# Feed-forward products on the unscaled input, with the token scale multiplied in when banks are emptied

## The chip, the core and the metric

The kernel runs on one core of a Trainium2 chip. The metric is the time of one execution on the device in microseconds (us). A core has five engines with a queue each: PE (TensorE) multiplies matrices, ACT (ScalarE) evaluates functions, DVE (VectorE) does elementwise work, POOL (GpSimd) does elementwise work and issues DMAs here, and SP only issues DMAs. They run side by side and wait for one another by semaphores.

## What is computed

Two layers of a decoder work on 256 prompt tokens and 8 x 8 sample tokens, 320 in all. What matters here is the end of a layer:

```python
x = x + rms_norm(merged @ w_o, g_mix_post)
h2 = rms_norm(x, g_ffn_pre)
f = (jax.nn.silu(h2 @ w_ffn_gate) * (h2 @ w_ffn_up)) @ w_ffn_down
x = x + rms_norm(f, g_ffn_post)
```

`rms_norm(x, g)` is `x * rsqrt(mean(x*x) + EPS) * g`: one scale for each token, one gain for each channel. The model width is 1024 and the feed-forward width is 2816, all in float32.

## The kernel before

**Layout.** Channels lie on the 128 partitions and the 320 tokens along the free dimension. `x` is 8 tiles of 128x320 (`KT` = 8), a feed-forward activation is 22 tiles (`FT` = 22). A matrix is cut into *units* of up to eight 128x128 weight tiles; the layer has 180, numbered in the order in which they are used: `U_WO` = 104 (8 units of `w_o`), `U_GU` = 112 (44 units, gate and up in turn), `U_DOWN` = 156 (24 units).

**Units.** Each unit's weights come by one 512 KB DMA from SP into one of four ring slots (`wring`). ACT rounds them to `whi`, DVE forms the rest `wlo = wring - whi`, and PE multiplies three ways (`whi*hi`, `whi*lo`, `wlo*hi`) for each of the eight tiles: 24 matmuls of 320 columns into one of banks 0 to 3. The activations are split likewise into `hhi` and `hlo`. `split(l, u)` on ACT and DVE prepares unit u + 3 (`AHEAD` = 3), so it also waits until PE has finished unit u - 1.

**The norm ahead of the feed-forward.** ACT squares the products of `w_o` (L888), PE averages the squares over channels with a matrix of ones into bank X (L449, L454), and ACT makes `rstd` from that with Ln and Exp (L774, L781). DVE multiplies the products with it and adds to `x`, two tiles at a time (L1374, L1376). ACT squares the new `x` (L992), PE averages again (L468 in `stat`), ACT makes the next `rstd`, DVE forms `acc = x * gain * rstd` (L1043 in `normalised`), ACT rounds this to `hhi` (L894), and DVE forms `hlo` (L1025 in `lower`). `keep_clock` (L444) issues matmuls whose result nobody reads, 20 ahead of the average and 12 behind it.

**The first units.** `first_units` works on units 0, 1 and 2 of `U_GU` together: for each k it waits until `h_ready` says that `hlo` tile k is there, and then issues nine matmuls. Unit 3 follows through `unit`, and then the loop over the other 40. I call them unit 0 to unit 43 of the feed-forward.

**The banks of the feed-forward.** For each n, ACT takes the sigmoid of the gate's bank (L793), DVE multiplies the bank with it (L1393), and then multiplies with the up projection's bank (L1399). The result is rounded to `fhi` (L999) and `flo`. Each engine's order is written out by hand, and so is every wait.

Of the kernel before, what the change touches and what calls it, by code (L numbers as in the profile page):

```python
# [53 lines left out]
ROPES, CONVS, POSTS = 12, TAPS, 16  # L54
# [34 lines left out]
def program(nc, w, xin, consts, params, r_in, c_in, x_out, rp_out, rs_out, cp_out, cs_out):  # L89
    ctx = ExitStack()  # L90
    with ctx:
# [101 lines left out]
        sq_paired = sem("sq_paired")  # L193
        stat_read = sem("stat_read")
# [60 lines left out]
        def _(pool):  # L255
# [137 lines left out]
            for n in range(0, KT, 2):  # L393

                pool.wait_ge(post_step, (DEPTH - 1) * POSTS + (8 + n + 2))
                pool.dma_start(x_out[:, n:n + 2, :], x[:, n:n + 2, :]).then_inc(x_stored, 16)
# [6 lines left out]
        def _(pe):  # L403
# [244 lines left out]
            for l in range(DEPTH):  # L648
# [75 lines left out]
                keep_clock(20)  # L724
                pe.wait_ge(stat_read, l * STATS + (ST_POST + 1))
                stat(l, 0, lambda k: sq8[:, k, :], KT, ones_d,
                     lambda k: pe.wait_ge(sq_done, l * SQS + (SQ_FFN + k + 1))).then_inc(stat_done, 1)

                keep_clock(12)
                first_units(l, U_GU // RING, lambda k: h_read(l, 8 + k))  # L730
                unit(l, U_GU // RING, AHEAD, AHEAD, h_tile)
# [22 lines left out]
        def _(act):  # L754
# [135 lines left out]
            def halves_of_h(l, sub):  # L890

                for k in range(KT):
                    act.wait_ge(h_value, l * 16 + (8 * sub + k + 1))
                    act.activation(hhi[:, k, :], acc[:, k, :], ACT.Copy).then_inc(h_hi, 1)  # L894
# [19 lines left out]
            for l in range(DEPTH):  # L914
                act.wait_ge(stat_done, l * STATS + 1)
                rsqrt(l, X[:, 0:T], 0, 0)
                halves_of_h(l, 0)
# [72 lines left out]
                for k in range(KT):  # L990
                    act.wait_ge(post_step, l * POSTS + (k // 2 * 2 + 2))
                    act.activation(sq8[:, k, :], x[:, k, :], ACT.Square).then_inc(sq_done, 1)  # L992
                act.wait_ge(stat_done, l * STATS + (ST_FFN + 1))
                rsqrt(l, X[:, 0:T], ST_FFN, RS_FFN)
                halves_of_h(l, 1)
# [5 lines left out]
                for n in range(FT):  # L1001
                    split(l, U_GU + 2 * n)
                    if n >= 4:
                        act.wait_ge(ffn_step, l * (2 * FT) + (2 * (n - 4) + 1))
                    gemm(l, U_GU + 2 * n)
                    sigmoid(sig[:, n % 4, :], bank[(2 * n) % 4][:, 0:T])
# [9 lines left out]
                for k in range(KT):  # L1016
                    act.wait_ge(post_step, l * POSTS + (8 + k // 2 * 2 + 2))
# [4 lines left out]
        def _(dve):  # L1022
# [15 lines left out]
            def normalised(l, sub, rs, gain):  # L1038

                dve.wait_ge(rstd_done, l * RSTDS + (rs + 1))  # L1040
                for k in range(KT + 2):
                    if k < KT:
                        dve.scalar_tensor_tensor(out=acc[:, k, :], in0=x[:, k, :], scalar=g_(gain + k), in1=rstd[:, :],  # L1043
                                                 op0=ALU.mult, op1=ALU.mult).then_inc(h_value, 1)
                    if k >= 2:
                        dve.wait_ge(h_hi, l * 16 + (8 * sub + k - 1))
# [202 lines left out]
            for l in range(DEPTH):  # L1249
                dve.wait_ge(par_loaded, l * 16 + 16)  # L1250
                normalised(l, 0, 0, G_MIXPRE)
# [107 lines left out]
                def post(sub, rs, sq0, gain, u0, ustep):  # L1359
# [145 lines left out]
```

## Time and profile before

| | |
|---|---|
| median of 3 runs | 1571.06 us (1570.09 to 1571.96) |
| profiled execution, its own time | 1572.03 us |
| span in the profile (first to last instruction) | 1570.2 us |
| PE busy | 1513.2 us, 96% |
| DVE busy | 1111.0 us, 71% |
| ACT busy | 674.3 us, 43% |
| POOL busy | 290.9 us, 19% |
| mean granted TensorE clock | 0.992 of full speed |

A busy PE may be doing nothing useful: the matmuls of `keep_clock` count as busy. The layers follow each other in time; the norm treated here stands at 541 to 555 us in the first and at 1309 to 1322 us in the second.

### The profile page before, as it was taken

Reading aid. Unit: us, or ns where it says so; the run is one execution under the profiler, and the core shown is the slowest. Engines: PE = TensorE matmul, PEld = TensorE weight load, DVE = VectorE, ACT = ScalarE, POOL = GpSimd, SP = SyncE. Lnnn points to the kernel's source line nnn. Section 1 sums busy time; section 2 is a strip of 40 time slices with the busy share of each in tenths; the row PEclk is TensorE's granted clock in tenths of the full one; section 3 lists DMA queues with packets and bytes.
Section 4 is the critical chain, followed back from the end, with each engine's and each line's share of the span. In section 5 each row is a group of like instructions: output and inputs, shape, how many; then the busy total and the mean of one; then the engine's idle time right before and its main releaser. Section 6 shows DMA issues by size and latency. Waiting matters only on the chain.

```text
span 1570.2 us, 25591 instructions
## 1 busy us (share of the span) xinstructions
PE 1513.2 (96%) x9840; PEld 1401.2 (89%) x9840; DVE 1111.0 (71%) x1735; ACT 674.3 (43%) x993; POOL 290.9 (19%) x257
## 2 busy tenths in 40 slices
PE   6999999999999999999999999999989999999997
PEld 5997878787899999999999978788779998999997
DVE  7789989987657567654466988989785665655544
ACT  3433434346355453434343344345454544443433
POOL 6974000101110029910000300101021000000000
PEclk8999999999999999999999999999999999999999
DMA  6554755646344434444444555748544442544443
GB/s 254 174 196 160 268 214 213 242 173 245 121 159 138 156 121 146 149 149 159 161 152 166 178 215 215 253 186 298 183 173 153 132 152 68 173 148 147 154 158 116
DMA packets 64541, 275.48 MB, mean 175 GB/s; under 512 B 7233, under 2 KB 7233, under 8 KB 55233
## 3 DMA queue, kind: packets, MB, share of 16 engines
q1 hardware_dynamic: 52560, 192.17, 36.7%
q0 software_dynamic: 11888, 82.04, 13.9%
q8 instruction: 62, 1.02, 0.3%
q14 instruction: 31, 0.25, 0.0%
HBM read 230.30 MB, written 43.89 MB: 175 GB/s over the span
## 4 chain that ended last, share of the span: by engine, by line
PE 82%; DVE 12%; ACT 4%; issue 1%; DMA 0%; DVEq 0%; ACTq 0%
PE bank L415 24%; PE bank L416 23%; PE bank L417 23%; DVE acc L1060 3%; DVE wlo L1025 2%; PE bank L602 2%; PE bank L580 1%; DVE state L1091 1%; PE bank L563 1%; PE bank L435 1%; DVE acc L1043 1%; ACT L770 1%; PE bank L516 1%; DVE tmp L1080 1%; DVE x L1376 1%
## 5 line engine op out<-in xcount | busy, mean ns | idle before, releaser
L415 PE MATMUL bank<-hhi,whi 128*128 128x320 f32 x2016 | 654.6, 325 | 7.8 <-DVE wlo L1025 7.8
L1025 DVE TENSOR_TENSOR wlo<-wring,whi 128x1024 fp32r<-128x1024 f32 x363 | 473.0, 1305 | 221.2 <-ACT whi L763 199.1
L417 PE MATMUL bank<-hhi,wlo 128*128 128x320 f32 x2016 | 625.7, 310 | 0.0
L416 PE MATMUL bank<-hlo,whi 128*128 128x320 f32 x2016 | 625.1, 310 | 0.0
L415 PEld LDWEIGHTS bank<-hhi,whi 128*128 128x128 f32 x2016 | 381.1, 189 | 39.3 <-issue 36.7
L416 PEld LDWEIGHTS bank<-hlo,whi 128*128 128x128 f32 x2016 | 381.4, 189 | 8.6 <-issue 7.7
L763 ACT ACTIVATE whi<-wring 128x1024 fp32r<-128x1024 f32 x264 | 278.1, 1055 | 240.5 <-PE bank L417 240.0
L417 PEld LDWEIGHTS bank<-hhi,wlo 128*128 128x128 f32 x2016 | 380.8, 189 | 0.0
L1060 DVE SCALAR_TENSOR_TENSOR acc<-up,par,acc 128x256 f32<-128x256 f32 x480 | 209.6, 504 | 0.2
L789 ACT ACTIVATE whi<-wring 128x1024 fp32r<-128x1024 f32 x96 | 101.2, 1054 | 72.1 <-PE bank L417 71.6
L793 ACT ACTIVATE sig<-bank 128x320 f32<-128x320 f32 x92 | 40.2, 437 | 202.0 <-PE bank L417 188.0
L415 PE MATMUL bank<-fhi,whi 128*128 128x320 f32 x352 | 110.4, 314 | 0.0
L417 PE MATMUL bank<-fhi,wlo 128*128 128x320 f32 x352 | 108.5, 308 | 0.0
L416 PE MATMUL bank<-flo,whi 128*128 128x320 f32 x352 | 108.5, 308 | 0.0
L1091 DVE SCALAR_TENSOR_TENSOR state<-state,con,bank 128x512 f32<-128x512 f32 x128 | 89.8, 743 | 12.5 <-PE bank L580 11.4
L299 POOL DMA_DIRECT2D rs_out<-state x32 | 17.4, 543 | 387.5 <-DVE state L1091 387.5
L392 POOL DMA_DIRECT2D par<-params x2 | 1.2, 578 | 465.0 <-DVE acc L1368 465.0
L415 PE MATMUL bank<-ghi,whi 128*128 128x320 f32 x256 | 78.9, 308 | 2.5 <-DVE glo L1025 2.5
L416 PE MATMUL bank<-glo,whi 128*128 128x320 f32 x256 | 78.8, 308 | 0.0
L417 PE MATMUL bank<-ghi,wlo 128*128 128x320 f32 x256 | 78.7, 308 | 0.0
L1393 DVE TENSOR_TENSOR tmp<-bank,sig 128x320 f32<-128x320 f32 x44 | 21.6, 491 | 70.5 <-ACT sig L793 70.5
L416 PEld LDWEIGHTS bank<-flo,whi 128*128 128x128 f32 x352 | 66.1, 188 | 0.6
(157 smaller groups left out, 1953.4 us busy)
## 6 DMA issues: line engine op xcount, KB each, us to landing
wring<-w SPq DMA_DIRECT2D x364, 512.0 KB, 3.7
state<-r_in POOLq DMA_DIRECT2D x32, 1024.0 KB, 7.6
rs_out<-state POOLq DMA_DIRECT2D x32, 1024.0 KB, 4.9
rp_out<-pst POOLq DMA_DIRECT2D x8, 512.0 KB, 7.7
us<-c_in POOLq DMA_DIRECT2D x2, 1216.0 KB, 5.5
cs_out<-us POOLq DMA_DIRECT2D x2, 1216.0 KB, 9.4
cp_out<-up POOLq DMA_DIRECT2D x2, 1144.0 KB, 5.9
con<-consts POOLq DMA_DIRECT2D x1, 1420.0 KB, 9.0
```

Source lines behind the costliest of these rows:

```text
L299: pool.dma_start(rs_out[H * QUADS + q], state[q % 2][:, :, :]).then_inc(r_stored[q % 2], 16)
L415: pe.matmul(bank[g][:, 0:T], whi[j][:, k, :], hi, start=start and k == 0, stop=False)
L416: pe.matmul(bank[g][:, 0:T], whi[j][:, k, :], lo, start=False, stop=False)
L417: mm = pe.matmul(bank[g][:, 0:T], wlo[j][:, k, :], hi, start=False, stop=stop and k == n - 1)
L602: mm = pe.matmul(aux[pos % 3][:, :], kdec[:, c, d * P:(d + 1) * P], vtok[:, c, :], start=(c == 0), stop=(c == 1))
L763: act.activation(whi[s][:, :, :], wring[s][:, :, :], ACT.Copy).then_inc(hi_done, 1)
L789: act.activation(whi[s][:, :, :], wring[s][:, :, :], ACT.Copy).then_inc(hi_done, 1)
L793: act.activation(dst, src, ACT.Sigmoid).then_inc(sig_done, 1)
L1025: return dve.tensor_tensor(dst, value, hi.bitcast(F32), ALU.subtract)
L1060: dve.scalar_tensor_tensor(out=out, in0=src, scalar=tap, in1=out, op0=ALU.mult, op1=ALU.add).then_inc(conv_step, 1)
L1091: dve.scalar_tensor_tensor(out=st, in0=st, scalar=con[:, ds(hd + C_CD, 1)], in1=aux[pos % 3][:, :], op0=ALU.mult, op1=ALU.add).then_inc(dv ...
L1393: dve.tensor_tensor(tmp[:, n % 4, :], bank[b][:, 0:T], sig[:, n % 4, :], ALU.mult).then_inc(ffn_step, 1)
```

## The change

Now the gain is multiplied into `x` on the way to `hhi` and `hlo`, and the scale of each token is left out of the products. A product of the feed-forward input is therefore too large or small by one factor for each token, and DVE multiplies this factor in when it reads the banks. Since the first units no longer need `rstd`, the squares are summed while they run.

The `x` update goes in groups of 1, 1, 2, 2 and 2 tiles. The eight averaging matmuls become four, since DVE first adds the squares in pairs (`add_squares`); two stand in `first_units` behind k = 5, two in unit 3 behind k = 3. The 20 `keep_clock` matmuls are gone and the 12 stay. The preparation of unit 3 moves ahead of the `x` groups on ACT, and behind them on DVE. The gate's Sigmoid becomes a Silu on an SBUF tile that DVE has scaled, and DVE has three operations for each n where it had two.

```diff
@@ -51,7 +51,10 @@
-ROPES, CONVS, POSTS = 12, TAPS, 16
+ROPES, CONVS, POSTS, POSTS0 = 12, TAPS, 18, 10
+MIX_GROUPS = ((0, 1), (1, 1), (2, 2), (4, 2), (6, 2))
@@ -437,6 +442,8 @@
                         mm = pe.matmul(bank[j][:, 0:T], wlo[j][:, k, :], hhi[:, k, :], start=False, stop=(k == UB - 1))
                         if k == UB - 1:
                             mm.then_inc(unit_done, 1)
+                    if between is not None:
+                        between(k)
             def keep_clock(n):
@@ -721,14 +728,19 @@
                          ready=(lambda k: pe.wait_ge(m_ready, l * 8 + (k + 1))) if n == 0 else None,
                          between=lambda k: square_means(l, 0, SQ_POST, n, k))
                 square_mean(l, SQ_POST, KT - 1).then_inc(stat_done, 1)
-                keep_clock(20)
-                pe.wait_ge(stat_read, l * STATS + (ST_POST + 1))
-                stat(l, 0, lambda k: sq8[:, k, :], KT, ones_d,
-                     lambda k: pe.wait_ge(sq_done, l * SQS + (SQ_FFN + k + 1))).then_inc(stat_done, 1)
                 keep_clock(12)
-                first_units(l, U_GU // RING, lambda k: h_read(l, 8 + k))
-                unit(l, U_GU // RING, AHEAD, AHEAD, h_tile)
+                def half_mean(i):
+                    pe.wait_ge(sq_halves, l * 2 + (i + 1))
+                    if i == 0:
+                        pe.wait_ge(stat_read, l * STATS + (ST_POST + 1))
+                    for k in (4 * i, 4 * i + 1):
+                        mm = pe.matmul(X[:, 0:T], ones_d[:, :], sq8[:, k, :], start=(k == 0), stop=(k == 5))
+                    return mm
+                first_units(l, U_GU // RING, lambda k: h_read(l, 8 + k), between=lambda k: half_mean(0) if k == 5 else None)
+                unit(l, U_GU // RING, AHEAD, AHEAD, h_tile, between=lambda k: half_mean(1).then_inc(stat_done, 1) if k == 3 else None)
                 with pe.Fori(1, FT // 2) as i:
                     for j in range(4):
                         pe.wait_ge(ffn_step, l * (2 * FT) + i * 4 + (j - 3))
@@ -987,23 +999,25 @@
                 squares_of_products(l, U_WO, 1, SQ_POST)
                 act.wait_ge(stat_done, l * STATS + (ST_POST + 1))
                 rsqrt(l, X[:, 0:T], ST_POST, RS_POST)
-                for k in range(KT):
-                    act.wait_ge(post_step, l * POSTS + (k // 2 * 2 + 2))
-                    act.activation(sq8[:, k, :], x[:, k, :], ACT.Square).then_inc(sq_done, 1)
+                split(l, U_GU)
+                for i, (k0, n) in enumerate(MIX_GROUPS):
+                    act.wait_ge(post_step, l * POSTS + (2 * i + 2))
+                    for k in range(k0, k0 + n):
+                        act.activation(hhi[:, k, :], x[:, k, :], ACT.Copy, scale=g_(G_FFNPRE + k)).then_inc(h_hi, 1)
+                    for k in range(k0, k0 + n):
+                        act.activation(sq8[:, k, :], x[:, k, :], ACT.Square).then_inc(sq_done, 1)
                 act.wait_ge(stat_done, l * STATS + (ST_FFN + 1))
                 rsqrt(l, X[:, 0:T], ST_FFN, RS_FFN)
-                halves_of_h(l, 1)
                 def f_half(n):
                     act.wait_ge(ffn_step, l * (2 * FT) + (2 * n + 2))
                     act.activation(fhi[:, n, :], tmp[:, n % 4, :], ACT.Copy).then_inc(f_hi, 1)
                 for n in range(FT):
-                    split(l, U_GU + 2 * n)
-                    if n >= 4:
-                        act.wait_ge(ffn_step, l * (2 * FT) + (2 * (n - 4) + 1))
-                    gemm(l, U_GU + 2 * n)
-                    sigmoid(sig[:, n % 4, :], bank[(2 * n) % 4][:, 0:T])
+                    if n:
+                        split(l, U_GU + 2 * n)
+                    act.wait_ge(ffn_step, l * (2 * FT) + (2 * n + 1))
+                    act.activation(sig[:, n % 4, :], sig[:, n % 4, :], ACT.Silu).then_inc(sig_done, 1)
                     if n:
                         f_half(n - 1)
                     split(l, U_GU + 2 * n + 1)
@@ -1368,38 +1382,64 @@
                         dve.tensor_scalar(acc[:, n, :], bank[n % 4][:, 0:T], g_(gain + n), None, ALU.mult).then_inc(y_copied, 1)
                     dve.wait_ge(rstd_done, l * RSTDS + (rs + 1))
                     dve.wait_ge(y_copied, l * 16 + (8 * sub + 8))
-                    scale = rstd[:, :].rearrange("p (o t) -> p o t", o=1).to_broadcast([P, 2, T])
-                    for n in range(0, KT, 2):
-                        y = tmp[:, n % 4:n % 4 + 2, :]
-                        dve.tensor_tensor(y, acc[:, n:n + 2, :], scale, ALU.mult).then_inc(post_step, 1)
-                        dve.wait_ge(post_step, l * POSTS + (8 * sub + n + 1))
-                        dve.tensor_tensor(x[:, n:n + 2, :], x[:, n:n + 2, :], y, ALU.add).then_inc(post_step, 1)
+                def x_group(l, step, k, n):
+                    y = tmp[:, k % 4:k % 4 + n, :]
+                    scale = rstd[:, :].rearrange("p (o t) -> p o t", o=1).to_broadcast([P, n, T])
+                    dve.tensor_tensor(y, acc[:, k:k + n, :], scale, ALU.mult).then_inc(post_step, 1)
+                    dve.wait_ge(post_step, l * POSTS + (step + 1))
+                    dve.tensor_tensor(x[:, k:k + n, :], x[:, k:k + n, :], y, ALU.add).then_inc(post_step, 1)
+                def x_low(k):
+                    dve.wait_ge(h_hi, l * 16 + (8 + k + 1))
+                    dve.scalar_tensor_tensor(out=hlo[:, k, :], in0=x[:, k, :], scalar=g_(G_FFNPRE + k), in1=hhi[:, k, :].bitcast(F32),
+                                             op0=ALU.mult, op1=ALU.subtract).then_inc(h_ready, 1)
+                def add_squares(i):
+                    dve.wait_ge(sq_done, l * SQS + (SQ_FFN + 4 * i + 4))
+                    dve.tensor_tensor(sq8[:, 4 * i:4 * i + 2, :], sq8[:, 4 * i:4 * i + 2, :], sq8[:, 4 * i + 2:4 * i + 4, :],
+                                      ALU.add).then_inc(sq_halves, 1)
                 post(0, RS_POST, SQ_POST, G_MIXPOST, U_WO, 1)
-                dve.wait_ge(post_step, l * POSTS + 8)
-                normalised(l, 1, RS_FFN, G_FFNPRE)
+                for i, (k, n) in enumerate(MIX_GROUPS):
+                    x_group(l, 2 * i, k, n)
+                    for low in ((), (0,), (1,), (2, 3), (4, 5, 6, 7))[i]:
+                        if low == 4:
+                            add_squares(0)
+                        x_low(low)
+                split(l, U_GU)
+                add_squares(1)
                 def ffn_low(n):
                     dve.wait_ge(f_hi, l * FT + (n + 1))
                     lower(flo[:, n, :], tmp[:, n % 4, :], fhi[:, n, :]).then_inc(f_ready, 1)
+                dve.wait_ge(rstd_done, l * RSTDS + (RS_FFN + 1))
                 for n in range(FT):
-                    split(l, U_GU + 2 * n)
+                    if n:
+                        split(l, U_GU + 2 * n)
                     b = (2 * n) % 4
-                    dve.wait_ge(sig_done, l * SIGS + (SIG_GATE + n + 1))
-                    if n >= 4:
-                        dve.wait_ge(f_ready, l * FT + (n - 3))
-                    dve.tensor_tensor(tmp[:, n % 4, :], bank[b][:, 0:T], sig[:, n % 4, :], ALU.mult).then_inc(ffn_step, 1)
+                    dve.wait_ge(unit_done, l * UNITS + (U_GU + 2 * n + 1))
+                    dve.tensor_tensor(sig[:, n % 4, :], bank[b][:, 0:T], rstd[:, :], ALU.mult).then_inc(ffn_step, 1)
                     if n:
                         ffn_low(n - 1)
                     split(l, U_GU + 2 * n + 1)
-                    dve.wait_ge(ffn_step, l * (2 * FT) + (2 * n + 1))
                     dve.wait_ge(unit_done, l * UNITS + (U_GU + 2 * n + 2))
-                    dve.tensor_tensor(tmp[:, n % 4, :], bank[b + 1][:, 0:T], tmp[:, n % 4, :], ALU.mult).then_inc(ffn_step, 1)
+                    if n >= 4:
+                        dve.wait_ge(f_ready, l * FT + (n - 3))
+                    dve.tensor_tensor(tmp[:, n % 4, :], bank[b + 1][:, 0:T], rstd[:, :], ALU.mult).then_inc(ffn_up, 1)
+                    dve.wait_ge(ffn_up, l * FT + (n + 1))
+                    dve.wait_ge(sig_done, l * SIGS + (SIG_GATE + n + 1))
+                    dve.tensor_tensor(tmp[:, n % 4, :], tmp[:, n % 4, :], sig[:, n % 4, :], ALU.mult).then_inc(ffn_step, 1)
                 ffn_low(FT - 1)
                 post(1, RS_POST2, SQ_POST2, G_FFNPOST, U_DOWN, 3)
-                dve.wait_ge(post_step, l * POSTS + 16)
+                for n in range(0, KT, 2):
+                    x_group(l, POSTS0 + n, n, 2)
+                dve.wait_ge(post_step, l * POSTS + POSTS)
                 dve.wait_ge(sample_conv_step, l * NEW_OPS + (SAMPLE_OPS + PAST_OPS))
```

What moves on the engines, in the first layer's passage from `w_o` to the feed-forward. On DVE, before: the `x` update (L1374, L1376), then `acc` (L1043) and `hlo` (L1025), then the gate's product (L1393).

```order
L1374 TENSOR_TENSOR tmp<-acc,rstd 128x640
L1376 TENSOR_TENSOR x<-x,tmp 128x640
L1043 SCALAR_TENSOR_TENSOR acc<-x,par,rstd 128x320 x3
L1025 TENSOR_TENSOR hlo<-acc,hhi 128x320
...
L1043 SCALAR_TENSOR_TENSOR acc<-x,par,rstd 128x320
L1025 TENSOR_TENSOR hlo<-acc,hhi 128x320 x3
L1025 TENSOR_TENSOR wlo_60<-wring_52,whi_56 128x1024
L1393 TENSOR_TENSOR tmp<-bank,sig 128x320
L1025 TENSOR_TENSOR wlo_57<-wring_49,whi_53 128x1024
```

And now, where L1390 and L1392 are the `x` update, L1397 is `x_low`, L1403 `add_squares`, L1426 the gate's scaling and L1039 what was L1025:

```order
L1390 TENSOR_TENSOR tmp<-acc,rstd 128x320
L1392 TENSOR_TENSOR x<-x,tmp 128x320
L1390 TENSOR_TENSOR tmp<-acc,rstd 128x320
L1392 TENSOR_TENSOR x<-x,tmp 128x320
L1397 SCALAR_TENSOR_TENSOR hlo<-x,par,hhi 128x320
...
L1403 TENSOR_TENSOR sq_81<-sq_81 128x640
L1397 SCALAR_TENSOR_TENSOR hlo<-x,par,hhi 128x320 x4
L1039 TENSOR_TENSOR wlo_60<-wring_52,whi_56 128x1024
L1403 TENSOR_TENSOR sq_81<-sq_81 128x640
L1426 TENSOR_TENSOR sig<-bank,rstd 128x320
L1039 TENSOR_TENSOR wlo_57<-wring_49,whi_53 128x1024
```

The first `hlo` follows two small groups where it followed the whole update and three rows of `acc`; `wlo_57`, the weights of unit 4, still follows the first reading of a gate's bank.

On ACT at the same place, before: Ln and Exp (L774, L781), `hhi` (L894), the weights of unit 3 (L763, `whi_56`), the table of Sigmoid, Sigmoid, and the weights of unit 4 (`whi_53`).

```order
L774 ACTIVATE lnv<-bank,eps 128x320
L781 ACTIVATE rstd<-lnv 128x320
L894 ACTIVATE hhi<-acc 128x320 x8
L763 ACTIVATE whi_56<-wring_52 128x1024
L793 ACT_TABLE_LOAD
L793 ACTIVATE sig<-bank 128x320
L763 ACTIVATE whi_53<-wring_49 128x1024
```

And now, from the last `hhi` (L1006) and squares (L1008) on:

```order
L1006 ACTIVATE hhi<-x,par 128x320 x2
L1008 ACTIVATE sq_81<-x 128x320 x2
L786 ACTIVATE lnv<-bank,eps 128x320
L793 ACTIVATE rstd<-lnv 128x320
L1020 ACT_TABLE_LOAD
L1020 ACTIVATE sig<-sig 128x320
L775 ACTIVATE whi_53<-wring_49 128x1024
```

Ln and Exp now stand directly ahead of the table load, the Silu and the weights of unit 4.

## Rows read from the trace of the kernel before

**Rows 1.** The page, part 4: chain that ended last, by engine.

```profile
PE 82%; DVE 12%; ACT 4%; issue 1%; DMA 0%; DVEq 0%; ACTq 0%
```

**Rows 2.** Timeline of PE, 540 to 572 us: start, length, instruction, idle before.

```profile
541.74 4.63 PE L444 MATMUL bank<-ones_d 128*128 128x128 f32 x40
...
550.02 1.34 PE L468 MATMUL bank<-sq,ones_d 128*128 128x320 f32 x4 [0.25 <-ACT sq L992]
...
554.57 0.39 PE L435 MATMUL bank<-hhi,whi 128*128 128x320 f32 x1 [0.52 <-DVE hlo L1025]
...
568.72 0.31 PE L415 MATMUL bank<-hhi,whi 128*128 128x320 f32 x1
```

**Rows 3.** Timeline of DVE, the same stretch.

```profile
543.00 0.83 DVE L1374 TENSOR_TENSOR tmp<-acc,rstd 128x640 f32<-128x640 f32 x1 [1.37 <-ACT rstd L781]
543.86 0.82 DVE L1376 TENSOR_TENSOR x<-x,tmp 128x640 f32<-128x640 f32 x1
544.60 0.82 DVE L1374 TENSOR_TENSOR tmp<-acc,rstd 128x640 f32<-128x640 f32 x1
...
553.93 0.48 DVE L1025 TENSOR_TENSOR hlo<-acc,hhi 128x320 fp32r<-128x320 f32 x1
554.34 0.55 DVE L1043 SCALAR_TENSOR_TENSOR acc<-x,par,rstd 128x320 f32<-128x320 f32 x1
...
565.93 1.23 DVE L1025 TENSOR_TENSOR wlo<-wring,whi 128x1024 fp32r<-128x1024 f32 x1 [0.46 <-ACT whi L763]
```

**Rows 4.** Timeline of ACT, 536 to 572 us.

```profile
542.50 0.47 ACT L781 ACTIVATE rstd<-lnv 128x320 f32<-128x320 f32 x1
...
551.41 0.53 ACT L774 ACTIVATE lnv<-bank,eps 128x320 f32<-128x320 f32 x1 [1.07 <-PE bank L468]
...
559.82 1.28 ACT L793 ACT_TABLE_LOAD   x1
564.52 0.44 ACT L793 ACTIVATE sig<-bank 128x320 f32<-128x320 f32 x1 [3.42 <-PE bank L437]
564.85 2.00 ACT L763 ACTIVATE whi<-wring 128x1024 fp32r<-128x1024 f32 x2
```

**Rows 5.** Timeline of PE, one averaging matmul (two rows) amid `w_o`.

```profile
535.38 0.70 PE L454 MATMUL bank<-sq,ones_d 128*128 128x320 f32 x2
...
536.06 0.31 PE L416 MATMUL bank<-hlo,whi 128*128 128x320 f32 x1
```

**Rows 6.** Timeline of PE, the same passage in the second layer.

```profile
1309.28 4.63 PE L444 MATMUL bank<-ones_d 128*128 128x128 f32 x40
...
1322.11 0.38 PE L435 MATMUL bank<-hhi,whi 128*128 128x320 f32 x1 [0.52 <-DVE hlo L1025]
```

**Rows 7.** Timeline of PE, one unit behind a wait.

```profile
403.22 0.38 PE L415 MATMUL bank<-hhi,whi 128*128 128x320 f32 x1 [3.82 <-DVE wlo L1025]
...
408.35 0.30 PE L415 MATMUL bank<-ghi,whi 128*128 128x320 f32 x1
```

**Rows 8.** Stretches: length, busy (instructions) of PE, PEld, DVE, ACT, POOL, granted clock, DMA, GB/s.

```profile
403.00:407.00 4.00, 3.78 (x16) 3.81 (x17) 4.00 (x5) 0.00 (x0) 3.92 (x2) 0.58 0.61 171
...
1171.00:1175.00 4.00, 4.00 (x19) 4.00 (x19) 4.00 (x4) 0.00 (x0) 3.92 (x2) 0.58 0.71 232
...
28.00:32.00 4.00, 1.73 (x10) 1.47 (x10) 4.00 (x4) 0.72 (x2) 3.76 (x4) 0.95 0.00 0
```

**Rows 9.** Timeline of ACT, a table load between two activations.

```profile
363.99 0.20 ACT L804 ACTIVATE rs<-rs 128x2 f32<-128x2 f32 x1
364.21 1.28 ACT L795 ACT_TABLE_LOAD   x1
365.50 0.53 ACT L795 ACTIVATE sgb<-bank,par 128x320 f32<-128x320 f32 x1
```

**Rows 10.** Groups of DVE by form, 620 to 640 us, while POOL works: mean ns.

```profile
L1025 DVE TENSOR_TENSOR wlo<-wring,whi 128x1024 fp32r<-128x1024 f32 x6 | 9.0, 1498 | 2.5 <-ACT whi L763 2.5
...
L1393 DVE TENSOR_TENSOR tmp<-bank,sig 128x320 f32<-128x320 f32 x3 | 1.5, 492 | 4.9 <-ACT sig L793 4.9
```

More of the change, by code:

```diff
@@ L193, in program @@
         sq_paired = sem("sq_paired")
+        sq_halves = sem("sq_halves")
+        ffn_up = sem("ffn_up")
         stat_read = sem("stat_read")
@@ L393, in _ @@
             for n in range(0, KT, 2):
-                pool.wait_ge(post_step, (DEPTH - 1) * POSTS + (8 + n + 2))
+                pool.wait_ge(post_step, (DEPTH - 1) * POSTS + (POSTS0 + n + 2))
                 pool.dma_start(x_out[:, n:n + 2, :], x[:, n:n + 2, :]).then_inc(x_stored, 16)
@@ L427, in _, with first_units @@
             h_tile = tile_of(hhi, hlo)
-            def first_units(l, q, ready):
+            def first_units(l, q, ready, between=None):
                 pe.wait_ge(lo_done, l * UNITS + (q * RING + AHEAD))
@@ L888, in squares_of_products, with halves_of_h @@
                     act.activation(sq8[:, n, :], bank[n % 4][:, 0:T], ACT.Square).then_inc(sq_done, 1)
-            def halves_of_h(l, sub):
+            def halves_of_h(l):
                 for k in range(KT):
-                    act.wait_ge(h_value, l * 16 + (8 * sub + k + 1))
+                    act.wait_ge(h_value, l * 8 + (k + 1))
                     act.activation(hhi[:, k, :], acc[:, k, :], ACT.Copy).then_inc(h_hi, 1)
@@ L916, in _ @@
                 rsqrt(l, X[:, 0:T], 0, 0)
-                halves_of_h(l, 0)
+                halves_of_h(l)
                 for n in range(KT):
@@ L1016, in _ @@
                 for k in range(KT):
-                    act.wait_ge(post_step, l * POSTS + (8 + k // 2 * 2 + 2))
+                    act.wait_ge(post_step, l * POSTS + (POSTS0 + k // 2 * 2 + 2))
                     act.activation(sq8[:, k, :], x[:, k, :], ACT.Square).then_inc(sq_done, 1)
@@ L1036, in split, with normalised @@
                 lower(wlo[s][:, :, :], wring[s][:, :, :], whi[s][:, :, :]).then_inc(lo_done, 1)
-            def normalised(l, sub, rs, gain):
-                dve.wait_ge(rstd_done, l * RSTDS + (rs + 1))
+            def normalised(l):
+                dve.wait_ge(rstd_done, l * RSTDS + 1)
                 for k in range(KT + 2):
                     if k < KT:
-                        dve.scalar_tensor_tensor(out=acc[:, k, :], in0=x[:, k, :], scalar=g_(gain + k), in1=rstd[:, :],
+                        dve.scalar_tensor_tensor(out=acc[:, k, :], in0=x[:, k, :], scalar=g_(G_MIXPRE + k), in1=rstd[:, :],
                                                  op0=ALU.mult, op1=ALU.mult).then_inc(h_value, 1)
                     if k >= 2:
-                        dve.wait_ge(h_hi, l * 16 + (8 * sub + k - 1))
+                        dve.wait_ge(h_hi, l * 16 + (k - 1))
                         lower(hlo[:, k - 2, :], acc[:, k - 2, :], hhi[:, k - 2, :]).then_inc(h_ready, 1)
@@ L1250, in _ @@
                 dve.wait_ge(par_loaded, l * 16 + 16)
-                normalised(l, 0, 0, G_MIXPRE)
+                normalised(l)
                 dve.memset(up[:, :, 0:PAD], 0.0).then_inc(pad_zeroed, 1)
```

## The prediction

> **What bounds the kernel now.** I read the page first: the chain that ended last is 82% PE and 12% DVE [rows 1], so the kernel is a stream of matmuls, and what an edit is worth is decided where PE waits. Then the timelines of PE, DVE and ACT around the norm ahead of the feed-forward. PE's part has to be read twice, because `keep_clock` fills most of the wait with matmuls that nobody needs. It starts at 541.74 us, when the last average of `w_o`'s squares is issued, and the first useful matmul of the feed-forward starts at 554.57 [rows 2]. So 12.83 us go by, of which the profile calls only 0.52 idle just before the end. The second layer has the same 12.83 us (1309.28 to 1322.11) [rows 6], so all that follows is counted twice.
>
> From 554.57 on PE doesn't stop. Unit 4, the first of the loop, starts at 568.72 [rows 2]: four units in 14.15 us, 3.52 us each after a first matmul that costs 0.07 more, or 0.147 for a matmul and 1.32 for one k of the three first units. The preparation of unit 4 is early: its `wlo` runs from 565.93 to 567.16 [rows 3], 1.5 us ahead of its use. Nothing downstream of this point is changed except for what happens beside PE, so **the start of unit 4 is where I settle the account**: the old one is 568.72.
>
> **What the change does, up to the first useful matmul.** `rstd` is ready at 542.97 [rows 4] and DVE starts at 543.00 [rows 3]. A 640-wide multiply is followed by its addition after 0.86, and this by the next group's multiply after 0.74. A 320-wide operation takes 0.48, and the next one starts 0.41 after its start if it doesn't depend on it [rows 3]; I take 0.51 where it does. The first group is then done at 543.99, the second at 544.91, and the first `x_low` starts at 544.84. It is a SCALAR_TENSOR_TENSOR like that of `acc`, 0.55 long with the next one 0.46 behind [rows 3], and ends at 545.39. Its `hhi` is in time: ACT's moved preparation of unit 3 (about 1.05, half of the 2.00 for two [rows 4]) ends near 543.9, and `hhi` takes about 0.5 from 544.03, between the 0.44 and 0.53 of ACT's rows on 320 columns [rows 4]. From the end of a `hlo` to PE it is 0.16 (554.41 to 554.57) [rows 2, 3]. The first useful matmul starts at 545.55, 9.0 us earlier than now.
>
> **That head start isn't kept,** since DVE now delivers the lows between the groups. Written out by the same pitches: multiply 545.30, addition 546.16, low of k = 1 to 547.45; multiply 547.36, addition 548.22, lows of k = 2 and 3 to 549.51 and 549.97; multiply 549.88, addition 550.74 to 551.56; `add_squares` of 0.82 to 552.30; lows of k = 4 to 7 from 552.77 at 0.46. PE starts k = 0 at 545.55, k = 1 at 547.61, k = 2 at 549.67, k = 3 behind it, and k = 4 at 552.93. It waits some 0.7 us three times. From k = 4 on PE is the slower one: four k of 1.32 end near 558.3.
>
> The averaging matmuls are not free where they now stand. One amid `w_o` shows its price: from 535.38 to 536.06 there are its two rows and one ordinary matmul, 0.68 less 0.15, so 0.53 [rows 5]. The two in the first units bring their end to 559.35. Unit 3 starts there. Its first four k take 1.76, the two averages behind them 1.07, and they are through, with 0.16 for the pipeline, at 562.35; unit 3 itself ends at 563.95.
>
> **Where the stall goes.** Now Ln (0.53) and Exp (0.47) [rows 4] run with 0.03 to 0.05 between, and `rstd` is there at 563.43. On DVE the gate's scaling waits for it, and behind it stands `wlo` of unit 4. On ACT the table load waits in line behind Exp, and behind it stand the Silu and `whi` of unit 4. In the kernel before, the load (559.82, 1.28 us) lay under the first units [rows 4]; that cover is gone. So: load to 564.73; the scaling (0.49 from a bank [rows 10]) is done at 563.95 and hidden by it; Silu, taken like Sigmoid, 0.44, to 565.18; `whi` starts 0.33 behind the Silu's start, as at 564.52 and 564.85 [rows 4], and ends at 566.14; `wlo` of 1.23 [rows 3] ends at 567.40; PE starts unit 4 at **567.56**. That is 1.16 us earlier than 568.72, and PE has waited 3.6 us ahead of it. Of 9.0 us, 6.7 went to the slower supply and the averages, and the rest mostly to this wait. Silu itself isn't in the trace; bounds are a Sigmoid's 0.44 and Ln's 0.53.
>
> Units 5 and 6 are safe: `whi` of unit 5 follows at once, its `wlo` ends near 569.4 behind the up scaling and the product, and it is due at 571.1; unit 6's ends near 573, due 574.6.
>
> **What such a wait costs in clock.** Ahead of 403.22 PE waited 3.82 us for a `wlo`; the granted clock over 403 to 407 is 0.58, so most of it at the lower level of 1.2 GHz, and the unit needs 5.13 us to 408.35 where 3.52 is normal [rows 7, 8]. That is 1.61. The same dip stands at 1171 to 1175, 0.58 with 19 matmul rows [rows 8]. My wait of 3.6 us is much like the first, so I take 1.61 for it; the bound below is 0, if the clock holds.
>
> **The sum** for a layer: -1.16 + 1.61 = +0.45, and for two +0.9. The profiled execution before took 1572.03 us, 0.97 above the median, so its like would be 1572.9, and against the median of 1571.06 I predict **1572.0 us**.
>
> **Beside the path.** DVE gets 44 more operations of 0.5 to 0.6 us, 22 in a layer. Two units take PE 7.03 us, and DVE's share of it is two `wlo`, one `flo` and three products. While POOL works in the first layer a `wlo` takes 1.50 instead of 1.23 and a reading of a bank 0.49 [rows 3, 10]. With the SBUF products at 0.48 x 1.5/1.23 = 0.59 this is 3.0 + 0.59 + 0.98 + 0.59 = 5.2 of 7.03: it is hidden by the matmuls. Without that cover it would be a microsecond for each n. Ring DMAs are issued by SP behind the same `wlo`, and the slot of unit 3 is free long before; I cost them at nothing. `keep_clock`'s 20 stood in a wait and save nothing by themselves.
>
> **Rivals.**
>
> *Faster.* The wait ahead of unit 4 is shorter than my chain and the clock holds. For: between groups PE still has work, and a load hidden by anything would leave 2.3 us of wait. Against: the table load stands in ACT's order right behind Exp. Time: -1.16 - 1.28 = -2.44 a layer, 1566.2. It decides for faster from 1.6 us a layer on. 10%. The clock alone holding gives -1.16 x 2 = -2.3 and 1568.8, within the same 0.2%: 8%.
>
> *Slower.* The clock falls already among the first groups. For: over 28 to 32 us PE, fed by DVE in the same way, is busy for 1.73 of 4.00 and the granted clock goes to 0.95, so it is at the lower level for a tenth of the stretch [rows 8]. Against: my gaps are 0.7, with 1.3 of work between them, and slowed matmuls would use up the gaps first. Full price another 1.61 a layer: +2.06, 1575.2. It decides from 1.1 us a layer of it on. 12%.
>
> *The table costs more than its row.* In the trace the load starts 0.02 behind the end of the activation ahead of it, lasts 1.28, and the next starts at once [rows 9]: 1.28 in all. If a wait as long as another load came with it, 1.28 more a layer, 1574.6: 4%. The Trainium skill ("ScalarE: Activation LUTs", What ACT_TABLE_LOAD costs) gives about 1.28 us for the load and about 1.38 us for a drain with every switch; by that page the sum would be 1574.8. Its first figure agrees with the row; its second doesn't show in it, so the rule gets the small chance that I gave the mechanism.
>
> *The feed-forward's own pace breaks* in the first layer, DVE needing over 7.03 us for two units. 1.8 us is missing for that; 0.3 for each of some 14 n under POOL gives +4 and 1576: 3%.
>
> **Numbers.** My forecast, with its own range of 1569 to 1574, has 63%. What one can tell from no change here is 0.2%, 3.1 us: 1567.9 to 1574.2. With the clock holding, and half a case of small errors either way, *same* gets 0.70, *faster* 0.11, *slower* 0.19. The range reaches from the case of the held clock to the price of two dips: 1568.2 to 1575.4.
>
> **What would show it.** First useful matmul near 545.6, 3.8 us behind the start of `keep_clock`; three gaps of 0.7; a wait of 3 to 4 us ahead of unit 4 on `wlo`, with the table load between Exp and Silu; a granted clock near 0.6 in the 4 us behind it, in both layers; unit 4 at 567.6, and PE without gaps for the rest of the feed-forward. I am wrong if the first lows come later than I chain them, if a table load is found elsewhere, if unit 4's weights are ready before unit 3 ends, or if gaps appear later on.

## The result, and the profile after

The changed kernel takes 1577.44 us (median of 7 runs, 1573.84 to 1578.16), the kernel before 1571.96 us beside it (7 runs, 1568.94 to 1573.45). The ratio is 1.0027, with a 95% interval of 1.0017 to 1.0036: slower, by some 4 us by the ratio and 5.5 by the two medians. The profiled execution is the one of 1577.44, with a span of 1575.6 us.

The page of the changed kernel, parts 1 and 4, in the lines for PE and DVE and the chain that ended last:

```profile
PE 1506.0 (96%) x9744; PEld 1392.1 (88%) x9744; DVE 1146.0 (73%) x1771; ACT 673.7 (43%) x993; POOL 288.7 (18%) x257
...
PE 75%; DVE 16%; ACT 4%; issue 2%; DVEq 0%; ACTq 0%
```

Against [rows 1] PE has given 7 points of the chain, DVE has gained 4. To see where, I measure each layer from the last average of `w_o`'s squares to the same place behind the down projection. These are PE rows of one kind, L449 before and L456 after. First the kernel before, then the changed one, from the timeline of PE:

```profile
541.09 0.81 PE L449 MATMUL bank<-sq,ones_d 128*128 128x320 f32 x2 [0.53 <-ACT sq L888]
...
789.80 0.81 PE L449 MATMUL bank<-sq,ones_d 128*128 128x320 f32 x2 [0.53 <-ACT sq L888]
```

```profile
538.97 0.81 PE L456 MATMUL bank<-sq,ones_d 128*128 128x320 f32 x2 [0.53 <-ACT sq L900]
543.43 0.39 PE L440 MATMUL bank<-hhi,whi 128*128 128x320 f32 x1 [0.98 <-DVE hlo L1397]
...
565.28 0.64 PE L420 MATMUL bank<-hhi,whi 128*128 128x320 f32 x1 [3.35 <-DVE wlo L1039]
...
568.57 0.31 PE L420 MATMUL bank<-hhi,whi 128*128 128x320 f32 x1
...
624.64 0.41 PE L420 MATMUL bank<-hhi,whi 128*128 128x320 f32 x1 [0.92 <-DVE wlo L1039]
633.07 0.42 PE L420 MATMUL bank<-hhi,whi 128*128 128x320 f32 x1 [1.10 <-DVE wlo L1039]
...
794.23 0.81 PE L456 MATMUL bank<-sq,ones_d 128*128 128x320 f32 x2 [0.53 <-ACT sq L900]
```

Before it is 248.71 us, after 255.26: **6.55 us more in the first layer**. In the second layer the same rows give 248.70 (1308.64 to 1557.34) and 248.92 (1313.80 to 1562.72), 0.22 more. The rest of the span is 1.4 us shorter, in parts that the change doesn't touch, and within the spread of the runs.

The passage that the prediction settled is as forecast. On ACT the load stands between Exp and Silu, as the timeline shows:

```profile
560.76 0.47 ACT L793 ACTIVATE rstd<-lnv 128x320 f32<-128x320 f32 x1
561.25 1.28 ACT L1020 ACT_TABLE_LOAD   x1
562.55 0.47 ACT L1020 ACTIVATE sig<-sig 128x320 f32<-128x320 f32 x1
562.92 1.99 ACT L775 ACTIVATE whi<-wring 128x1024 fp32r<-128x1024 f32 x2
```

From the average to unit 4's first matmul it is 26.31 us (538.97 to 565.28); before, 27.63 (541.09 to 568.72, [rows 2]). So unit 4 starts 1.3 us earlier, behind a wait of 3.35. Then the matmuls stand 0.27 apart until the 13th of the unit starts at 568.57, 3.29 behind the first where 1.83 is normal: 1.46 us for the lower of the two clocks. The stretches show the dip:

```profile
564.00:568.00 4.00, 2.72 (x10) 2.73 (x11) 3.65 (x5) 1.19 (x2) 0.00 (x0) 0.63 0.39 124
568.00:572.00 4.00, 4.00 (x28) 4.00 (x27) 2.92 (x5) 2.44 (x4) 0.00 (x0) 0.94 0.48 146
...
1340.00:1344.00 4.00, 3.89 (x17) 3.89 (x18) 2.97 (x6) 1.45 (x3) 0.00 (x0) 0.59 0.56 171
```

What wasn't forecast are six waits from 616.42 us on, each on a `wlo` and mostly some 8.3 us apart, which is two units and a stall (two of them are shown above). The profile counts 4.68 us of idle for the six. The number of matmuls tells more: these are the 20 us stretches of the changed kernel beside POOL's work, then one of the kernel before.

```profile
577.00:597.00 20.00, 20.00 (x138) 20.00 (x137) 17.23 (x16) 7.34 (x12) 18.74 (x12) 1.00 0.46 148
597.00:617.00 20.00, 19.83 (x136) 19.57 (x135) 18.10 (x16) 6.43 (x10) 19.06 (x13) 1.00 0.34 115
617.00:637.00 20.00, 17.98 (x120) 17.40 (x120) 18.11 (x15) 5.46 (x8) 19.06 (x13) 1.00 0.40 131
637.00:657.00 20.00, 17.97 (x120) 17.24 (x118) 17.26 (x14) 8.20 (x12) 18.98 (x14) 1.00 0.39 131
657.00:677.00 20.00, 19.54 (x134) 19.48 (x134) 15.91 (x21) 8.19 (x12) 11.95 (x12) 1.00 0.49 157
```

```profile
617.00:637.00 20.00, 20.00 (x138) 20.00 (x138) 12.81 (x15) 7.82 (x12) 19.14 (x12) 1.00 0.46 148
```

The first column in brackets counts PE's rows: 648 in the five stretches, and 692 in those of before. The 44 that are missing are 6.5 us at 0.147; such a count can be off by a row or two, and what the first layer lost beyond the second's 0.22 is 6.33 us. So this is the whole difference. The clock is at 1.00, so it isn't that. DVE is busy for 18.11 of 20 us where it was for 12.81, and POOL works all the time in both. One n of it, from DVE's timeline of the changed kernel (L1434 up scaling, L1437 product, L1426 gate scaling, L1039 `wlo` and `flo`):

```profile
624.51 0.48 DVE L1434 TENSOR_TENSOR tmp<-bank,rstd 128x320 f32<-128x320 f32 x1
625.02 1.06 DVE L1437 TENSOR_TENSOR tmp<-tmp,sig 128x320 f32<-128x320 f32 x1
626.01 2.12 DVE L1039 TENSOR_TENSOR wlo<-wring,whi 128x1024 fp32r<-128x1024 f32 x1
628.05 0.48 DVE L1426 TENSOR_TENSOR sig<-bank,rstd 128x320 f32<-128x320 f32 x1
629.42 1.35 DVE L1039 TENSOR_TENSOR flo<-tmp,fhi 128x320 fp32r<-128x320 f32 x1 [0.90 <-ACT fhi L1014]
630.70 2.32 DVE L1039 TENSOR_TENSOR wlo<-wring,whi 128x1024 fp32r<-128x1024 f32 x1
632.94 0.48 DVE L1434 TENSOR_TENSOR tmp<-bank,rstd 128x320 f32<-128x320 f32 x1
```

The readers of a bank take 0.48, as ever. What has both inputs in SBUF takes 1.06, 2.12, 1.35 and 2.32 us, against 0.49, 1.23, 0.49 and 1.23 in the second layer, where POOL is still. And in the middle DVE stands idle for 0.90 us, waiting for `fhi`. The period is 8.43 us here, and 8.33 in the mean of this stretch, where PE needs 7.03.

### The profile page after: what moved, and what is told of

Read it like the earlier page. It is cut to its first block, busy times and chain, and to the rows that moved or that the text cites. A ratio compares the mean times of both kernels' runs of the same rounds, so it can differ in the third digit from the quotient of the medians.

```text
span 1575.6 us, 25399 instructions
## 1 busy us (share of the span) xinstructions
PE 1506.0 (96%) x9744; PEld 1392.1 (88%) x9744; DVE 1146.0 (73%) x1771; ACT 673.7 (43%) x993; POOL 288.7 (18%) x257
## 4 chain that ended last, share of the span: by engine, by line
PE 75%; DVE 16%; ACT 4%; issue 2%; DVEq 0%; ACTq 0%
PE bank L420 22%; PE bank L421 21%; PE bank L422 21%; DVE wlo L1039 5%; DVE acc L1074 3%; PE bank L609 2%; PE bank L587 1%; PE bank L570 1%; DVE tmp L1094 1%; DVE state L1105 1%; DVE x L1392 1%; PE bank L523 1%; ACT L782 1%; DVE tmp L1390 1%; PE bank L552 1%
## 5 line engine op out<-in xcount | busy, mean ns | idle before, releaser
L1039 DVE TENSOR_TENSOR wlo<-wring,whi 128x1024 fp32r<-128x1024 f32 x363 | 481.9, 1330 | 206.8 <-ACT whi L775 182.3
L1020 ACT ACTIVATE sig<-sig 128x320 f32<-128x320 f32 x44 | 20.8, 472 | 147.9 <-DVE sig L1426 147.8
L420 PEld LDWEIGHTS bank<-fhi,whi 128*128 128x128 f32 x352 | 66.1, 188 | 0.6
```

The costliest lines, as they stand in the source:

```text
L420: pe.matmul(bank[g][:, 0:T], whi[j][:, k, :], hi, start=start and k == 0, stop=False)
L1020: act.activation(sig[:, n % 4, :], sig[:, n % 4, :], ACT.Silu).then_inc(sig_done, 1)
L1039: return dve.tensor_tensor(dst, value, hi.bitcast(F32), ALU.subtract)
```

## The experiments

Two things are in question: what the period of 8.4 us is made of, and whether the account of the wait ahead of unit 4 holds. The rival theories of the first: POOL and DVE get in each other's way when both read SBUF (P); the number of DVE operations counts, whatever they read (N, or C for the chain of them); contention and DVE's own idle time are both needed (S, which I added after e7). All runs were timed beside the kernel before; each ratio below is to it. The last two columns are the layers' lengths from the rows of the same kind as above.

| | median us | ratio, 95% interval | first layer | second |
|---|---|---|---|---|
| before (profile above) | | | 248.71 | 248.70 |
| changed | 1577.44 | 1.0027 (1.0017 to 1.0036) | 255.26 | 248.92 |
| e1 changed, few taps on POOL | 1570.48 | 0.9998 (0.9990 to 1.0007) | 248.95 | 249.02 |
| e2 before, few taps on POOL | 1571.23 | 0.9998 (0.9989 to 1.0007) | 248.70 | 248.71 |
| e3 product read from bank | 1569.90 | 0.9991 (0.9982 to 1.0000) | 249.02 | 249.03 |
| e4 unit 4 early | 1569.50 | 0.9993 (0.9984 to 1.0002) | 253.14 | 244.14 |
| e5 both, e3 and e4 | 1560.25 | 0.9943 (0.9928 to 0.9957) | 244.12 | 244.11 |
| e6 clock kept | 1575.55 | 1.0038 (1.0024 to 1.0053) | 255.22 | 247.51 |
| e7 before, extra SBUF operation | 1569.92 | 0.9996 (0.9987 to 1.0006) | 248.70 | 248.71 |
| e8 before, extra bank operation | 1569.81 | 0.9997 (0.9988 to 1.0006) | 248.71 | 248.70 |
| e9 `fhi` ahead of Silu | 1570.94 | 0.9997 (0.9989 to 1.0006) | 249.01 | 249.01 |
| e10 both, e9 and e4 | 1560.43 | 0.9935 (0.9922 to 0.9949) | 244.13 | 244.12 |

The runs of one kernel spread over 2 to 6 us (1573.84 to 1578.16 for the changed one). The layers' lengths come from one profiled execution of each kernel, but agree within 0.11 us from kernel to kernel where nothing sets them apart, and they carry the verdicts.

**e1 and e2: POOL's taps cut to one eighth, in the changed kernel and in the one before.** Seven of eight channel tiles of the second layer's sample convolution are left out.

```diff
-past_taps(l + 1, past, ptap, cw[:, 0:KT], cw[:, KT:KT * (1 + TAPS)])
+past_taps(l + 1, past, ptap, cw[:, 0:KT], cw[:, KT:KT * (1 + TAPS)], tiles=1)
```

> The changed kernel, in which POOL's taps for the second layer's sample convolution (they run beside the first layer's feed-forward) work on one of eight channel tiles; the other seven are left out. Theory P (POOL and DVE get in each other's way when both read SBUF): DVE's wlo in the first layer's feed-forward goes back from 2.1-2.3 us to 1.23, PE's waits of about 1 us there vanish, and the kernel is some 6 us faster than the changed kernel, so about 1571. Theory C (the chain of three products and the late flo is too long for DVE by itself): the waits stay, within 1 us of the changed kernel.

> The kernel before with the same seven eighths of POOL's taps left out. Both theories: PE has no wait in this feed-forward before, so nothing is gained, within 1 us of the kernel before; wlo goes from 1.5 to 1.23 us. A gain of several us would mean that POOL costs time in another way than through DVE, and the previous run would show nothing about DVE.

Both came out as theory P has it: the first layer of the changed kernel falls by 6.31 us to 248.95, `wlo` takes 1.23 us again (1.24 in the mean while POOL's short operations still run), and the kernel before gains nothing. So POOL is needed for the loss, and C falls. It doesn't say yet which of DVE's operations it hits.

**e3: the product reads the bank.**

```diff
-dve.tensor_tensor(tmp[:, n % 4, :], bank[b + 1][:, 0:T], rstd[:, :], ALU.mult).then_inc(ffn_up, 1)
+dve.tensor_tensor(bank[b + 1][:, 0:T], bank[b + 1][:, 0:T], rstd[:, :], ALU.mult).then_inc(ffn_up, 1)
-dve.tensor_tensor(tmp[:, n % 4, :], tmp[:, n % 4, :], sig[:, n % 4, :], ALU.mult).then_inc(ffn_step, 1)
+dve.tensor_tensor(tmp[:, n % 4, :], bank[b + 1][:, 0:T], sig[:, n % 4, :], ALU.mult).then_inc(ffn_step, 1)
```

> The changed kernel, but the scaled up projection is written back into its bank and the product reads it from there: the same number of DVE operations, one fewer with both inputs in SBUF. Theory P: the product takes 0.49 us instead of 0.9, the wlo beside it get shorter, PE's waits in the first layer's feed-forward shrink from 4.5 us in sum to under 1, and the kernel is 4 to 6 us faster than the changed one. Theory N (the number of DVE operations beside POOL counts, whatever they read): no change, within 1 us.

DVE's groups in this run from 600 to 655 us; the figures behind the bar are busy us and mean ns:

```profile
L1039 DVE TENSOR_TENSOR wlo<-wring,whi 128x1024 fp32r<-128x1024 f32 x16 | 28.3, 1767 | 0.0
L1039 DVE TENSOR_TENSOR flo<-tmp,fhi 128x320 fp32r<-128x320 f32 x8 | 10.9, 1362 | 7.2 <-ACT fhi L1014 7.2
L1437 DVE TENSOR_TENSOR tmp<-bank,sig 128x320 f32<-128x320 f32 x8 | 3.9, 492 | 0.3
```

The same number of operations, one with two SBUF inputs fewer, and 6.24 us are gone from the first layer: N falls. The product's own time falls by some 0.45 us, and the mean `wlo` by another 0.45 (2.22 in the changed kernel's same stretch). DVE's 0.90 us of waiting for `fhi` in each n is still there.

**e7 and e8: an extra operation in the kernel before.**

```diff
+dve.tensor_tensor(acc[:, n % 8, :], x[:, n % 8, :], rstd[:, :], ALU.mult)            # e7
+dve.tensor_tensor(acc[:, n % 8, :], bank[b + 1][:, 0:T], rstd[:, :], ALU.mult)      # e8
 dve.tensor_tensor(tmp[:, n % 4, :], bank[b + 1][:, 0:T], tmp[:, n % 4, :], ALU.mult).then_inc(ffn_step, 1)
```

> The kernel before with one more DVE operation for each n of the feed-forward, x times rstd into a tile that nobody reads: both inputs in SBUF, 22 in a layer. Theory P: beside POOL it takes about 0.9 us and makes the wlo around it longer; DVE then needs 8.4 us for two units and the first layer's feed-forward gets waits of about 1 us, in sum 4 to 7 us slower than the kernel before; the second layer stays as it was. Theory N (the operations only fill idle time): no change in either layer.

> The kernel before with the same extra operation, but with the up projection's bank as its first input. Theory P: 0.49 us each, no waits in either layer, within 1 us of the kernel before. If the number of operations beside POOL is what counts: as slow as the run with the SBUF input.

e8 came out as expected. e7 did not: I expected 4 to 7 us, and there is nothing, 248.70 and 248.71. Yet its operations beside POOL are nearly as long as the changed kernel's: 6.56 us for the four with two SBUF inputs, against 6.85. From its DVE timeline:

```profile
628.68 0.48 DVE L1393 TENSOR_TENSOR tmp<-bank,sig 128x320 f32<-128x320 f32 x1
629.08 1.18 DVE L1025 TENSOR_TENSOR flo<-tmp,fhi 128x320 fp32r<-128x320 f32 x1
630.18 2.08 DVE L1025 TENSOR_TENSOR wlo<-wring,whi 128x1024 fp32r<-128x1024 f32 x1
632.19 1.58 DVE L1399 TENSOR_TENSOR acc<-x,rstd 128x320 f32<-128x320 f32 x1
633.70 0.48 DVE L1400 TENSOR_TENSOR tmp<-bank,tmp 128x320 f32<-128x320 f32 x1
634.10 1.72 DVE L1025 TENSOR_TENSOR wlo<-wring,whi 128x1024 fp32r<-128x1024 f32 x1
635.74 0.48 DVE L1393 TENSOR_TENSOR tmp<-bank,sig 128x320 f32<-128x320 f32 x1
```

The same four operations with two SBUF inputs and two readers of a bank as in the changed kernel, and the period is 7.06 us: DVE is full to the brim, without idle time from 597 to 657 us. So theory P alone fell here. What the changed kernel has beside it is the 0.90 us for `fhi`.

**e9: `fhi` of the last n ahead of this n's Silu.**

```diff
+                    if n:
+                        f_half(n - 1)
                     act.wait_ge(ffn_step, l * (2 * FT) + (2 * n + 1))
                     act.activation(sig[:, n % 4, :], sig[:, n % 4, :], ACT.Silu).then_inc(sig_done, 1)
-                    if n:
-                        f_half(n - 1)
```

> The changed kernel, but ACT rounds the last n's product to fhi ahead of this n's Silu, not behind it, so that flo doesn't stop DVE for 0.9 us for each n. The run with an extra SBUF operation in the kernel before had no waits, with DVE 100% busy beside POOL. Theory S (the changed kernel's period of 8.3 us comes from both: operations that queue behind POOL's, and 0.9 us of DVE standing idle for fhi in each n): the period falls to 7.1 to 7.5, the waits of PE in the first layer's feed-forward shrink from 6.4 us in all to under 2, and the kernel is 4 to 6 us faster than the changed one, near 1572. Theory P alone (only the number of operations with two SBUF inputs counts): the waits stay, within 1.5 us of the changed kernel.

Theory S has it. DVE's timeline of this run, one n:

```profile
619.58 0.49 DVE L1426 TENSOR_TENSOR sig<-bank,rstd 128x320 f32<-128x320 f32 x1
619.99 1.02 DVE L1039 TENSOR_TENSOR flo<-tmp,fhi 128x320 fp32r<-128x320 f32 x1
621.56 1.50 DVE L1039 TENSOR_TENSOR wlo<-wring,whi 128x1024 fp32r<-128x1024 f32 x1 [0.55 <-ACT whi L775]
623.10 0.49 DVE L1434 TENSOR_TENSOR tmp<-bank,rstd 128x320 f32<-128x320 f32 x1
623.63 0.94 DVE L1437 TENSOR_TENSOR tmp<-tmp,sig 128x320 f32<-128x320 f32 x1
624.49 2.08 DVE L1039 TENSOR_TENSOR wlo<-wring,whi 128x1024 fp32r<-128x1024 f32 x1
626.62 0.49 DVE L1426 TENSOR_TENSOR sig<-bank,rstd 128x320 f32<-128x320 f32 x1
```

The period is 7.04 us, PE has no wait left there, and the first layer takes 249.01. All operations of the changed kernel are still in it, and POOL's too. Either cause taken away is enough.

**What the two causes have in common** stands in POOL's rows. These are all that start in the n of the changed kernel shown above, 624.51 to 632.94:

```profile
625.81 1.23 POOL L277 TENSOR_TENSOR ptap<-us,cw 128x512 f32<-128x512 f32 x1
627.12 2.16 POOL L280 TENSOR_TENSOR past<-past,ptap 128x512 f32<-128x512 f32 x1
629.36 1.07 POOL L277 TENSOR_TENSOR ptap<-us,cw 128x512 f32<-128x512 f32 x1
630.51 1.43 POOL L280 TENSOR_TENSOR past<-past,ptap 128x512 f32<-128x512 f32 x1
632.01 1.97 POOL L277 TENSOR_TENSOR ptap<-us,cw 128x512 f32<-128x512 f32 x1
```

And two of e9's:

```profile
620.73 1.24 POOL L277 TENSOR_TENSOR ptap<-us,cw 128x512 f32<-128x512 f32 x1
624.29 1.20 POOL L277 TENSOR_TENSOR ptap<-us,cw 128x512 f32<-128x512 f32 x1
```

The changed kernel's `wlo` of 626.01 starts while POOL's first operation runs. That one ends at 627.04, and `wlo` at 628.13, 1.09 behind it. All 14 `wlo` of this kernel from 596 to 655 us end 1.07 to 1.09 us behind the end of the POOL operation during which they started, and all 15 `flo` and products 0.34 to 0.36 behind it; in e9 and e7 the same figures come back. Alone these operations take 1.23 and 0.49. So such an operation lasts as long as what is left of POOL's, and then 1.08 or 0.35 us. That is why `wlo` takes 1.50 and 2.08 us by turns in e9: the first starts 0.41 us ahead of the end of POOL's operation, the second 1.00.

The period follows from how many POOL operations fall into it. The changed kernel has five in each of its periods of 8.2 to 8.4 us, and e9, e7 and e3 have four in each of theirs of some 7 us. My reading is that POOL fits a fifth one in while DVE waits for `fhi` and reads a bank, and that DVE's next operation then waits for that one: this would be why 0.90 us of idle time costs 1.3 to 1.4 us of period. No run varied POOL's operations by themselves, so this last step is argued and not shown.

**e4: unit 4 prepared early.** On ACT `split(l, U_GU + 1)` moves ahead of the wait for the average, on DVE ahead of the wait for `rstd`.

```diff
                 split(l, U_GU)
                 add_squares(1)
+                split(l, U_GU + 1)
 ...
                     if n:
                         ffn_low(n - 1)
-                    split(l, U_GU + 2 * n + 1)
+                        split(l, U_GU + 2 * n + 1)
```

> The changed kernel, but the preparation of unit 4 stands ahead of Ln on ACT and ahead of the wait for rstd on DVE. My account of the passage: the wait of 3.35 us ahead of unit 4 goes in both layers, and with it the dip of the clock (1.6 each), so 2 x 4.9 = 9.8 us faster than the changed kernel, near 1567.5. Rival (the Silu and its table are what unit 5 then waits for): a new wait of 1 to 2 us ahead of unit 5, and only 5 to 7 us faster.

In the second layer it is as my account has it: 4.78 us less than in the changed kernel, which is the wait of 3.35 and the clock's 1.46, and no wait ahead of unit 5. The first layer gets 2.12 of that. Its waits beside POOL now begin at 596.94 and are eight where they were six; PE arrived earlier at a stretch in which DVE sets the pace. So the sum is 6.90 us and not 9.8: it lies where the rival had it, but not by the rival's mechanism.

**e5 and e10: that and a mend of the first layer.**

> Both mends in one: unit 4 prepared early and the product read from its bank. If the two costs are apart, each layer from the last average of w_o to that of the down projection takes 244.1 us where the kernel before takes 248.7 (the second layer of the run with unit 4 early alone shows it), so 9 us less than the kernel before: 1562. Rival: with the product mended DVE's wlo still takes 1.77 us beside POOL, and the first layer had no need of the slack yet; then waits come back there and 1 to 4 us of the gain are lost.

> The same exchange together with the early preparation of unit 4, the product still read from SBUF. Theory S: like the run with both mends, 1560 to 1563, as far as the period of DVE beside POOL comes down to 7.03 us; if it stops at 7.4, some 1 to 4 us are lost in the first layer and nothing in the second.

Now the two gains add up, 244.1 in both layers and in both versions, and each kernel is some 10 us faster than the one before by the medians (9.2 by the layers), at ratios of 0.9943 and 0.9935. e5's stretch 617 to 637 shows PE without a gap and the clock full:

```profile
617.00:637.00 20.00, 20.00 (x138) 20.00 (x137) 17.20 (x18) 8.19 (x12) 19.06 (x13) 1.00 0.44 147
```

**e6: matmuls without use in the wait ahead of unit 4.**

```diff
+                keep_clock(12)
                 with pe.Fori(1, FT // 2) as i:
```

> The changed kernel with 12 matmuls without use (2.8 us) behind unit 3, in the wait ahead of unit 4; nothing else is changed. If the wait's second price is the clock's dip and nothing more, the wait shrinks to 0.5 us as the profile counts it, unit 4 starts at the same distance from w_o's end, and its 24 matmuls take 3.5 us instead of about 5.1: 3.2 us less in both layers together. Rival (what follows the wait is slow for another reason, such as the weights' loads): no change. In the first layer POOL's stretch may take some of it back, as DVE sets the pace there; so 1.6 to 3.2 us.

PE's timeline and a stretch of this run:

```profile
561.00 2.84 PE L451 MATMUL bank<-ones_d 128*128 128x128 f32 x24
564.51 0.41 PE L420 MATMUL bank<-hhi,whi 128*128 128x320 f32 x1 [0.68 <-DVE wlo L1040]
```

```profile
564.00:568.00 4.00, 3.48 (x24) 3.49 (x25) 3.07 (x6) 1.19 (x4) 0.00 (x0) 1.00 0.50 145
```

Unit 4 starts at the same distance as without them, 26.29 us behind 538.22, and the clock stays full. The second layer gains 1.41 us, the dip's price. The first gains 0.04: what PE saves it waits away beside POOL, as in e4. So the sum is 1.45 and not the 1.6 to 3.2 that I gave, and the ratio can't be told from the changed kernel's.

## Why the prediction was wrong

The forecast was 1572.0 us with a range to 1575.4, and "same" at 0.70; it came out at 1577.44 and slower. Each layer was to grow by 0.45 us; the second grew by 0.22, the first by 6.55.

- **The first useful matmul** was right: 4.46 us behind the last average (538.97 to 543.43), and I had the same from 541.09 to 545.55.
- **The supply between groups** was right in shape: waits of 0.41, 0.47 and 0.35 us where I had some 0.7, since the profile counts a wait from the modelled end of a matmul.
- **The wait ahead of unit 4** was right: 1.16 us earlier was forecast, 1.32 measured; the wait 3.6, and 3.35 by the profile. Only my split of the 9.0 us was added up wrongly: by the prediction's own times 4.2 us and not 6.7 go to the slower supply and the averages, and 3.6 to the wait. Measured, it is 4.2 and 3.5. The table load lies where I put it and costs 1.28; the drain that the Trainium skill ("ScalarE: Activation LUTs", What ACT_TABLE_LOAD costs) adds to it doesn't show here either.
- **The clock's price** was right in kind, 1.61 against 1.46, and e6 shows it by itself. The sum for the second layer was +0.45 and is +0.22.
- **The step that failed is the pace of the feed-forward beside POOL.** I wrote that DVE's share of two units was 5.2 of 7.03 us and hidden, by scaling the old mean of `wlo` (1.50 us) to the new product. Those means belonged to an order in which DVE had idle time to spare: from 600 to 650 us of the kernel before, one `wlo` of each n took 1.7 to 2.0 us and the other 1.2 to 1.4, where in the changed kernel both take 2.1 to 2.3. In the changed kernel four operations with two SBUF inputs take 6.85 us, two readers of a bank 0.96, and DVE's wait for `fhi` 0.90: 8.71 us, of which neighbours overlap by some tenths, and the period is 8.43. So the operations alone were under-sized, 5.2 for 7.8 us, and the wait was left out altogether: ACT rounds `fhi` behind the Silu, which now waits for DVE's gate scaling, and I chained this for n = 0 alone, where there is no `flo`. I had this as the last rival at 3%, with a price of 4 us; it was 6.3.

The Trainium skill ("SBUF — State Buffer", Who interferes with whom) has a rule that I should have weighed: a VectorE instruction with two SBUF inputs and a GpSimd instruction that reads SBUF contend, and the second to be issued waits for all of the first; with at most one SBUF input, outside VectorE's 2-port modes, there is no contention. The runs agree: 0.48 to 0.49 us for each reader of a bank beside POOL, 0.8 to 2.3 for the others, the fixed 1.08 and 0.35 us behind the end of POOL's operation, and e3 against the changed kernel. The page doesn't say what such waits add up to; that was 6.3 us or nothing, depending on the 0.90 us that e9 removes.

What stays open is whether the fifth POOL operation of each period is by itself what turns 0.90 us of idle time into 1.3 to 1.4.

## What to carry to other kernels

A saving on the path buys a place in the queue of the next bound. Here 9.0 us of earlier start became 1.3 at the first unit of the loop. The slower supply and the averages took 4.2 of it, and 3.5 went to a wait, because the weights of that unit were prepared behind the value that the start no longer needed; preparing them ahead of it gave back 4.8 us in the second layer, and 4.9 in the first once its pace was mended (e3 against e5, e9 against e10). When operations are added to an engine that "has time", write out one whole period of it with its waits on the other engines, in the stretch where a neighbour shares its memory path, and not a sum of old means.

## What the runs showed of the hardware that I had not expected

- A DVE operation with two SBUF inputs that starts during one of POOL's ends a fixed time behind it, 1.08 us for 1024 columns and 0.35 for 320: the same 320-column subtraction took 0.49 us alone, 1.02 to 1.18 in the rows of e9 and e7 shown here, and 1.35 in the changed kernel. Even so DVE at 100% busy (e7) cost nothing at all, and DVE at 90% with a wait in each period cost 6.3 us.
- A PE wait costs more than the profile's idle figure: 4.68 us counted for the six waits, 6.3 lost. Each hides 0.16 us, since a matmul's row is 0.31 long where the next starts 0.147 behind it, and the second matmul behind a wait starts 0.25 behind the first, 0.10 late. Six times 0.26 makes up the difference of 1.6.
